# Merge stage of a bidirectional encoder: w_out loaded from two queues, and the first tile turned and copied among the squares

## The reference, cut to what matters

```python
def rms_norm(x, g):
    xf = x.astype(jnp.float32)
    y = xf * lax.rsqrt(jnp.mean(xf * xf, axis=-1, keepdims=True) + EPS)
    return (y * g.astype(jnp.float32)).astype(x.dtype)

def trunk(x):
    u = rms_norm(x, attn_norm[l]) @ w_in[l]
    y_h = hyena_mixer(u[..., :COL_HYENA], ...)
    y_a = mla_mixer(u[..., COL_HYENA:COL_Q], u[..., COL_Q:COL_KV], u[..., COL_KV:], ...)
    y = jnp.concatenate([y_h, y_a], axis=-1).reshape(B, L, 2, D_MIX // 2)
    y = rms_norm(y, out_norm[l].reshape(2, D_MIX // 2)).reshape(B, L, D_MIX)
    x = x + y @ w_out[l]
    x = x + ec_moe(rms_norm(x, mlp_norm[l]), w_router[l], w_gate[l], w_up[l], w_down[l])
    return x
```

## Time and profile before

| | us |
|---|---|
| median of 3 runs | 2941.3 |
| lowest and highest of them | 2938.06, 2942.07 |
| the profiled execution | 2940.52 |
| its span, first to last instruction | 2938.5 |
| the merge, from its first transfer to the next stage's first | 1781.0 to 2102.4 |

### The profile page before, as it was taken

One profiled execution on the slowest core, in us unless ns is written; L12 is line 12 of the kernel. 1 busy time (PEld: TensorE's weight loads), 2 busy tenths in 40 slices (PEclk: granted clock), 3 DMA queues, 4 the chain that ended last, 5 costly groups with the idle time before them and its releaser, 6 DMA issues. The chain is left out here.

```text
span 2938.5 us, 45637 instructions
## 1 busy us (share of the span) xinstructions
PE 2579.2 (88%) x16813; PEld 1444.9 (49%) x16813; DVE 1912.9 (65%) x2737; ACT 1660.0 (56%) x2708; POOL 1055.4 (36%) x984
## 2 busy tenths in 40 slices
PE   7899999859999999978989896999502999999998
PEld 4455555425555555543332332555302666666664
DVE  5455555458888888868979895444396454545552
ACT  6634444349999999978548554333321454545440
POOL 1221211148888888867009101212020112222221
PEclk9999999969999999989999997999755999999999
DMA  7423333335211101136978795544511667666762
GB/s 185 117 60 90 88 103 84 85 74 186 75 37 35 28 21 37 38 87 250 307 245 273 271 313 171 161 146 140 182 57 39 185 223 235 194 193 204 233 179 33
DMA packets 268924, 415.99 MB, mean 142 GB/s; under 512 B 55390, under 2 KB 148958, under 8 KB 267168
## 3 DMA queue, kind: packets, MB, share of 16 engines
q1 hardware_dynamic: 219696, 344.39, 36.1%
q0 software_dynamic: 10752, 37.75, 5.5%
q10 hardware_dynamic: 38288, 31.37, 3.8%
HBM read 280.56 MB, written 132.86 MB: 141 GB/s over the span
## 5 line engine op out<-in xcount | busy, mean ns | idle before, releaser
L1162 POOL TENSOR_TENSOR at_p<-at_pf,at_p 128x512 f16<-128x512 f32 x424 | 510.8, 1214 | 136.3 <-ACT at_p L1296 109.6
L1424 DVE TENSOR_REDUCE at_mxs<-at_pM 128x1 f32<-128x512 f32 x512 | 342.2, 684 | 72.4 <-PE at_pM L1323 62.0
L1295 ACT ACTIVATE at_pf<-at_pS,at_scale 128x512 f32<-128x512 f32 x520 | 359.4, 691 | 28.0 <-PE at_pS L1348 27.2
L1296 ACT ACTIVATE at_p<-at_pS,at_scale 128x512 f16<-128x512 f32 x520 | 356.7, 686 | 0.0
L1367 PEld LDWEIGHTS at_pO<-at_vv,at_p 128*128 128x128 f16 x4160 | 233.4, 97 | 140.5 <-POOL at_p L1162 31.9
L1367 PE MATMUL at_pO<-at_vv,at_p 128*128 128x129 f16 x4160 | 267.4, 207 | 8.4 <-POOL at_p L1162 6.5
L3007 PE MATMUL ex_pY<-mo_down,ex_hT 128*128 128x512 f32 x512 | 224.0, 595 | 0.0
L1323 PE MATMUL at_pM<-at_k,at_q 96*128 96x512 f16 x512 | 189.5, 389 | 28.1 <-DVE at_q L1410 17.5
L1346 PE MATMUL at_pS<-at_q,at_k 97*128 97x512 f16 (+1 forms) x528 | 199.7, 378 | 3.9 <-issue 2.2
L1347 PE MATMUL at_pS<-at_q,at_k 96*128 96x512 f16 (+1 forms) x528 | 199.5, 378 | 0.0
L1348 PE MATMUL at_pS<-at_q,at_k 96*128 96x512 f16 (+1 forms) x528 | 198.4, 376 | 0.0
(11 more groups left out here) (351 smaller groups left out, 5911.0 us busy)
## 6 DMA issues: line engine op xcount, KB each, us to landing
sp_rows<-s_F SPq DMA_DIRECT2D x76, 512.0 KB, 5.5
s_F<-fs_a SPq DMA_DIRECT2D x72, 512.0 KB, 3.1
mo_raw<-in_w_gate SPq DMA_DIRECT2D x32, 1024.0 KB, 7.5
mo_raw<-in_w_up SPq DMA_DIRECT2D x32, 1024.0 KB, 7.5
mo_down<-in_w_down SPq DMA_DIRECT2D x16, 2048.0 KB
s_G<-sp_gg SPq DMA_DIRECT2D x72, 256.0 KB, 4.1
sp_tab<-tab_spec SPq DMA_DIRECT2D x76, 224.0 KB, 3.9
s_QK<-pj_R ACTq DMA_DIRECT2D x18, 768.0 KB, 4.7
```

Of the source, the lines that this page charges most:

```text
L1162: eng.tensor_tensor(p2[r][:, :], pf[:, r, :], p1[r][:, :], ALU.subtract).then_inc(own_done if n in own else others_done, 1)
L1295: act.activation(pf[:, n % 4, :], pS[n % 2][:, 0:QB], ACT.Exp, scale=scale[:, 0:1])
L1296: act.activation(p1[n % 4][:, :], pS[n % 2][:, 0:QB], ACT.Exp, scale=scale[:, 0:1]).then_inc(pS_free, 1)
L1424: dve.tensor_reduce(mxs[:, j // NC, j % NC:j % NC + 1], pM[j % 2][:, :], AX.X, ALU.max).then_inc(pM_free, 1)
```

## The change

- The 16 loads of w_out are no longer issued by SP ahead of G of tile 1. SP issues G of tile 1 right behind the gain, and then the eight odd pieces. ACT issues the eight even pieces as the first thing that it does in the merge.
- ACT no longer starts with `square_y(0)`. It waits for the gain, squares pieces 0 to 3, then does `square_y(0)`, then pieces 4 to 10, then `copy_yT(0)`, then pieces 11 to 15. Behind piece 15 the scale follows at once.
- PE turns tile 0 before it inverts tile 1.
- DVE does `leave_y(0)` before `close(1)`.

```diff
+        def load_w(eng, i):
+            k, h = divmod(i, 2)
+            eng.dma_start(places[i], io["w_out"][0, k * P:(k + 1) * P, h * 512:(h + 1) * 512]).then_inc(w_in[i], 16)
...
             sp.dma_start(ogain[:, :], io["out_norm"]).then_inc(gain_in, 16)
-            for i in range(PIECES):
-                k, h = divmod(i, 2)
-                sp.dma_start(places[i], io["w_out"][0, k * P:(k + 1) * P, h * 512:(h + 1) * 512]).then_inc(w_in[i], 16)
             load_g(1)
+            for i in range(1, PIECES, 2):
+                load_w(sp, i)
             load_a(1)
...
-            square_y(0)
+            for i in range(0, PIECES, 2):
+                load_w(act, i)
             act.wait_ge(gain_in, 16)
             for i in range(PIECES):
+
+                if i == 4:
+                    square_y(0)
+                if i == 11:
+                    copy_yT(0)
...
-            copy_yT(0)
             act.wait_ge(w_summed, 1)
...
             invert(0)
-            invert(1)
             pe.wait_ge(eye_in, 16)
             turn_y(0)
+            invert(1)
             pe.wait_ge(consts, 4)
             pe.wait_ge(w_squared, PIECES)
...
             norm_y(0)
+            leave_y(0)
             close(1)
-            leave_y(0)
```

## The result

The changed kernel took 2945.08 us (median of 12 runs, 2942.38 to 2949.36), the kernel before 2942.16 us beside it (12 runs, 2937.34 to 2945.10). The ratio is 1.0016, with a 95% interval of 1.0008 to 1.0023. So the change makes the kernel slower by some 2 to 7 us; the medians stand 2.9 us apart. The forecast was +3.0 us, with a range of 2938.5 to 2948.

What follows compares the result with a forecast made beforehand. Taken to bound the kernel: the start of the first wH (1806.97). The gap shrinks by 2.4 us, but squares begin 2.9 later and carry 2.4 more: +3.0 us on 2940.5 gives 2943.5 us, range 2938.5 to 2948.

Steps and rivals of the forecast that it cites:

- What bounds the kernel now: Start of the merge: 4.59 us from the last sum to the first wH, to shrink to 2.2, -2.4 us.
- Everything behind the first `wH` at fixed distance: Merge behind the first wH: tiles run at PE's rate without slack, so what shifts the first wH shifts the end.
- What decides is piece 1: ACT takes pieces in order, so all hangs on piece 1, first of SP's half; break-even if landed by 1791.6.
- Piece 1 at 1794.6: Landing of SP's first piece, some 3900 KB through: 1795.3 less 0.7 us that a second queue can fill early.
- nothing filled: Upper bound for piece 1's landing, the second queue filling no idle DMA time: 1795.3.
- Equal turns: DMA engines serve both full queues half each, so SP's 1860 KB pass with nearly all of ACT's 2048 KB.
- a whole transfer's share in one turn: Alternative on the DMA queues: seven even pieces pass, 3652 KB, piece 1 about 1793.9, sum +2.3 for +3.0.
- ACT's work behind piece 1: ACT from piece 1's landing to the last sum: squares, square_y(0), copies and a 0.2 us wait, 13.17 us.
- Piece 1 early: SP's queue gets well over half, piece 1 at 1789.8: -1.8 us, 2938.7; chance 0.19 together with no effect.
- Two streams slowing each other: Reading w_out in two streams beside G at 284 GB/s: piece 1 at 1797.4, 2946.3 to 2947.7; chance 0.09.
- The clock: PE may begin produce(0) at 1.2 GHz, costing nothing itself; a low stretch costs 1.4 us: 2942.1 or 2944.9.
- The signs: Changed profile: first square near 1788 to 1791, then a gap of 3 us or more on ACT; first wH at 1810.0.

Runs made afterwards that it cites:

- queues_alone: Kernel before with only the transfers split over two queues, old engine order; M (merge's first transfer issue on SP to first wH on ACT) 27.20 us.
- act_held: Changed kernel, but ACT issues its eight pieces only when the gain has landed; M 29.92 us.
- again_before: The kernel before run once more, unchanged; M 25.24 us (25.94 in the first trace).
- mixed_queue: One queue, new engine order, gain first, pieces 0 to 2 mixed among SP's early transfers, G of tile 1 behind piece 9; M 24.93 us, ratio 0.9990.
- halves: Changed kernel with pieces 0 to 7 on ACT's queue and 8 to 15 on SP's; M 26.20 us.
- g1_behind: Changed kernel with G of tile 1 behind SP's eight odd pieces in place of ahead of them; M 26.99 us.
- g1_ahead_one_queue: Changed kernel with all 16 pieces on SP's queue, in order, behind G of tile 1; M 24.19 us.
- again_after: The changed kernel run once more, unchanged; M 29.52 us (29.54 in the first trace).

## Why the prediction was right, step by step

- **What bounds the kernel now** was read rightly. With the new order on ACT, PE and DVE and the old transfers (`order_alone`) the time from the last sum to the first `wH` fell from 4.59 to 2.50 us, where 2.2 were forecast. The last sum itself came 0.5 us earlier (20.85 against 21.35), as the squares start 2.9 us sooner and carry `square_y(0)` and the copies. The order on PE was not tried by itself on one queue.
- **Everything behind the first `wH` at fixed distance**: 16.50 and 16.51 us to the turn of tile 1 in both kernels, though `produce(0)` began at half clock in the changed one (below). From the first `wH` to the next stage's first transfer were 295.7 us in nine of the fourteen traces, M 23.35 to 29.65. The other five had 294.8 (`queues_alone`), 295.4 (before), 295.8 (`act_held`) and twice 296.9 (`again_before` and `mixed_queue`, the two with a long low stretch of the clock, see the last section). So M was a sound measure.
- **What decides is piece 1**: shown by `halves`, `g1_behind` and `g1_ahead_one_queue`, three kernels whose M came within about 0.1 us of what was expected from counting packets and from the changed kernel's own rows. Not every expectation held so well: `act_held` was 2.8 us off and `mixed_queue` 1.5.
- **Piece 1 at 1794.6, that is at 13.6**: it came at 14.4. It is the largest miss, and the term that was mis-sized is the 0.7 us that a second queue was to fill at the start. The windows row of the changed kernel for the same 3 us, counted from the merge's first issue, answers to the first of rows 4:

```profile
1784.65:1787.65 3.00, 0.00 (x0) 0.00 (x0) 0.00 (x0) 0.00 (x0) 0.00 (x0) 0.50 0.87 268
```

  The engines' busy share did rise, from 0.77 to 0.87, but they moved 268 GB/s in place of 261: each packet took about a tenth longer. The upper bound of the prediction, nothing filled, 14.3, was nearer. That bound is itself read 0.15 us late, because the issue times of single pieces in it (and in the caption of rows 7) are from the mean spacing of 0.53 us. By its own row piece 10 of the kernel before was issued at 1788.55 and landed at 1795.15, at 14.1 (13.9 in `again_before`). So the same bytes took 14.2 to 14.4 us on two queues and 13.9 to 14.1 on one.
- **Equal turns** held in packets where both queues had work, and not in the first 5 us. In bytes SP got less than half while its small packets were through; that made the gain late (10.4 against 6.8), which the prediction had not counted. It cost nothing here, since piece 1 came later still. The Trainium skill ("DMA: Bandwidth & Descriptors", "Queues, rings and completion order") lets each engine take turns by packets of several descriptors. The version that the prediction priced, a whole transfer's share in one turn, would have piece 1 0.7 us ahead of where equal turns have it; piece 1 came no earlier than equal turns have it. The counts speak against that version too. G of tile 1 has 256 rows of 2 KB and a piece of w_out 128, so turns of whole transfers would give SP's queue two packets for one while G goes. From 1793.28 to 1794.88, while it went, they were even:

```profile
q1 hardware_dynamic: 176, 0.33, 53.6%
q10 hardware_dynamic: 173, 0.32, 51.9%
```

  Whether a turn is one row or a few, the counts can't tell. The other rule of the Trainium skill, in the same page's section "Issuing engines are not separate DMA queues", is that a second issuing engine saves only issue time. In bytes the trace agrees: 4.02 MB by 13.0 us against 3.97.
- **ACT's work behind piece 1**, 13.17: measured 13.1 (1798.08 to 1811.21). The wait before the copies was 0.16, forecast 0.2. The scale took 2.0, forecast 2.2: PE's clock was already up when it summed the squares. In `again_after`, where it was not, the scale took 2.2.
- **The rivals.** Piece 1 early did not happen. Two streams slowing each other to 284 GB/s did not either: 309 GB/s in the mean of the first 13.0 us, where the kernel before had 305, and 388 from 1794.65 to 1797.65. The clock did what its paragraph said for `produce(0)` and not what it said for tile 1.
- **The signs.** The first square came at 1794.10, which is 10.4, and the forecast's 1788 to 1791 is 7 to 10; that is the late gain again. G of tile 0 landed 0.9 us later (4.6 after its issue against 3.7), 1.4 were forecast. No gap stood before another odd piece.

The clock, from the windows of the changed kernel (length, busy us of PE, PEld, DVE, ACT and POOL, granted clock, DMA share, GB/s):

```profile
1809.20:1812.60 3.40, 1.25 (x6) 0.49 (x6) 0.72 (x2) 2.28 (x8) 0.41 (x2) 0.97 1.07 279
1812.60:1819.40 6.80, 4.80 (x13) 1.58 (x12) 5.41 (x11) 5.49 (x8) 0.32 (x1) 0.51 0.09 33
1819.40:1826.00 6.60, 6.60 (x32) 3.04 (x31) 6.09 (x10) 6.06 (x11) 0.00 (x0) 1.00 0.00 0
```

The clock rose at 1809.0 behind the turn and `invert(1)`, fell at 1812.4 and rose again at 1819.2 (the granted clock's own records; the windows above lie some 0.2 us later), so the first 4.2 us of `produce(0)` (from 1814.96) ran at 1.2 GHz. PE then had no idle time until it had caught up with DVE, and the turn of tile 1 was not late.

So the sum closes in M: +3.0, plus 0.8 for piece 1, less 0.2 for the scale, is +3.6, which is what the first pair of traces shows. The mechanism was right and the size a little small. That the medians of the whole time stand just 2.9 us apart is in part luck: the merge shows 3.6 and 4.3 in M and 3.1 to 3.9 in its length, and the interval of the ratio, 2.4 to 6.8 us, holds both.

## What to carry to other kernels

Where an engine takes pieces in a fixed order, count for the first piece that it needs how many packets stand ahead of it on its own queue, and add as many for a second full queue: in these traces two full queues got equal numbers of packets, and all together no more bytes than one queue. Deal pieces out so that the order of landing is the order of use, or leave them on one queue. And look for the wait that is only there because of an instruction's place: a new order on three engines, with the turn ahead of a matmul that waits for a late transfer, gained 1.9 to 2.6 us in M without a change to any transfer. But judge an order together with the transfers it runs beside. The same order cost 2.3 us once piece 1 came late, since it moved work from ahead of the awaited piece to behind it.

## What the runs showed of the hardware

**Two full queues get equal numbers of packets, whatever the packets' size.** With both queues full the packets came out as 293 to 294 (2 KB on ACT's side, mostly 32 and 512 bytes on SP's) and as 226 to 228 (2 KB on ACT's, partly 4 KB on SP's). A 4 KB transfer, the gain, landed 8.4 us after its issue beside ACT's queue of 2 KB packets, and 4.9 without it.

**A low stretch of the clock of 3.4 us cost nothing, and one of 6.8 us more than 1 us.** Before, the clock was low from 1824.0 to 1827.4, and the turn of tile 2 came 15.10 us behind that of tile 1 (1838.58 - 1823.48); in the changed kernel, with no low stretch there, 15.09 (1844.81 - 1829.72). In `again_after` it was low from 1829.37 to 1832.78, and the distance was 15.08. The 1.4 us that the prediction put on such a stretch were not there. In the second execution of the kernel before it was low for twice as long:

```profile
1822.00:1828.90 6.90, 6.35 (x19) 2.80 (x20) 5.57 (x8) 3.45 (x8) 1.40 (x3) 0.51 0.40 107
```

and its turns of tiles 1 and 2 stood 16.35 us apart:

```profile
1822.44 1.97 PE L2371 MATMUL mg_pY<-mg_eye,mg_yn 128*128 128x128 f32 x8 [2.56 <-DVE mg_yn L2450]
...
1838.79 1.04 PE L2371 MATMUL mg_pY<-mg_eye,mg_yn 128*128 128x128 f32 x8
```

In `mixed_queue` the clock was low from 1822.50 to 1829.33, and the turns stood 17.14 us apart. To the next stage both kernels took 1.2 us more behind the first `wH` than most. So one kernel's merge is more than 1 us longer or not by how long its clock stays down there. Together with the scatter ahead of the merge this can hide a change of 2 us, which M shows at once, in single whole times.
